# Hyena stage of a two-block transformer kernel: spectrum products in two PSUM banks, two inverse blocks side by side, signal parts block by block

## The reference

```python
def hyena(zh, p):
    B, L, _ = zh.shape                      # 1, 512, 3 * 512
    zc = cw[0] * zp[:, :-2] + cw[1] * zp[:, 1:-1] + cw[2] * zp[:, 2:] + p['hy_conv_b']
    v, x1, x2 = jnp.split(zc.astype(jnp.float32), 3, axis=-1)
    kf = jnp.fft.rfft(hyena_filters(L, p), axis=0)
    y = v
    for o, gate in enumerate((x1, x2)):
        yf = jnp.fft.rfft(y, n=2 * L, axis=1)
        conv = jnp.fft.irfft(yf * kf[:, o][None], n=2 * L, axis=1)[:, :L]
        y = gate * (conv + skip[o] * y)
    return y.astype(zh.dtype)
```

## Time and profile before

| | us |
|---|---|
| median of 3 runs | 3689.84 (3687.9 to 3692.53) |
| the profiled execution, its time | 3695.89 |
| its span, first to last instruction | 3694.1 |
| TensorE busy | 3524.5 (95% of the span) |
| DVE busy | 2093.1 (57%) |
| ACT busy | 1383.3 (37%) |
| POOL busy | 1831.8 (50%) |
| first product of the Hyena projection to last inverse product | some 1800 to 1983 |

### The profile page before, as it was taken

One profiled execution on the slowest core, in us unless ns is written; L12 is line 12 of the kernel. 1 busy time (PEld: TensorE's weight loads), 2 busy tenths in 40 slices (PEclk: granted clock), 3 DMA queues, 4 the chain that ended last, 5 costly groups with the idle time before them and its releaser, 6 DMA issues. The chain is left out here.

```text
span 3694.1 us, 49775 instructions
## 1 busy us (share of the span) xinstructions
PE 3524.5 (95%) x17547; PEld 2994.5 (81%) x17547; DVE 2093.1 (57%) x4197; ACT 1383.3 (37%) x1941; POOL 1831.8 (50%) x909
## 2 busy tenths in 40 slices
PE   8999997999999999999989999899999999999999
PEld 5777766777777688776767776689999999999999
DVE  4553045222224344215865355459999997677776
ACT  4333234223244332223323444323345454444443
POOL 5667433223243244343333311345666666788886
PEclk9999998999999999999999999999999999999999
DMA  6997545444467289422424312694459999899996
GB/s 237 367 369 259 170 148 155 129 151 142 151 202 245 86 259 288 159 86 91 142 75 137 97 60 86 221 342 158 161 179 316 346 346 348 329 378 392 387 383 233
DMA packets 458130, 813.81 MB, mean 220 GB/s; under 512 B 31544, under 2 KB 308984, under 8 KB 455322
## 3 DMA queue, kind: packets, MB, share of 16 engines
q1 hardware_dynamic: 278416, 436.07, 35.9%
q10 hardware_dynamic: 142666, 241.11, 18.5%
q0 software_dynamic: 36864, 134.23, 9.6%
HBM read 682.84 MB, written 195.56 MB: 238 GB/s over the span
## 5 line engine op out<-in xcount | busy, mean ns | idle before, releaser
L549 POOL TENSOR_TENSOR weights_lo<-weights_raw,weights_hi 128x1024 fp32r<-128x1024 f32 x649 | 1586.8, 2450 | 1791.4 <-ACT weights_hi L1241 1665.6
L627 PE MATMUL bank<-operand_hi,weights_hi 128*128 128x512 f32 (+1 forms) x2856 | 1094.5, 383 | 51.5 <-DVE operand_lo L1985 18.1
L629 PE MATMUL bank<-operand_hi,weights_lo 128*128 128x512 f32 (+1 forms) x2856 | 1065.5, 373 | 0.0
L628 PE MATMUL bank<-operand_lo,weights_hi 128*128 128x512 f32 (+1 forms) x2856 | 1064.7, 373 | 0.0
L1241 ACT ACTIVATE weights_hi<-weights_raw 128x1024 fp32r<-128x1024 f32 x649 | 683.3, 1056 | 850.0 <-PE bank L629 530.5
L627 PEld LDWEIGHTS bank<-operand_hi,weights_hi 128*128 128x128 f32 x2856 | 542.7, 190 | 141.6 <-DVE operand_lo L1985 20.2
L628 PEld LDWEIGHTS bank<-operand_lo,weights_hi 128*128 128x128 f32 x2856 | 543.2, 190 | 74.8 <-issue 5.5
L629 PEld LDWEIGHTS bank<-operand_hi,weights_lo 128*128 128x128 f32 x2856 | 541.1, 189 | 74.7
L627 PE MATMUL bank<-expert_hi,weights_hi 128*128 128x384 f32 x1024 | 345.1, 337 | 0.0
L629 PE MATMUL bank<-expert_hi,weights_lo 128*128 128x384 f32 x1024 | 345.0, 337 | 0.0
L628 PE MATMUL bank<-expert_lo,weights_hi 128*128 128x384 f32 x1024 | 345.0, 337 | 0.0
(11 more groups left out here) (401 smaller groups left out, 4883.9 us busy)
## 6 DMA issues: line engine op xcount, KB each, us to landing
weights_raw<-in_w_ffn_gu SPq DMA_DIRECT2D x132, 512.0 KB
expert_table_v<-in_w_peer_out SPq DMA_DIRECT2D x120, 512.0 KB, 5.3
weights_raw<-in_w_peer_ahead SPq DMA_DIRECT2D x120, 512.0 KB
weights_raw<-in_w_peer_out SPq DMA_DIRECT2D x120, 512.0 KB
expert_table_u<-expert_turned ACTq DMA_DIRECT2D x360, 128.0 KB, 4.7
expert_rows<-in_w_peer_ahead ACTq DMA_DIRECT2D x82, 512.0 KB, 6.8
peer_gates<-gate_stage SPq DMA_DIRECT2D x24, 1024.0 KB
expert_gates<-peer_gates ACTq DMA_DIRECT2D x16, 1536.0 KB
```

The lines of the kernel that those rows point to most:

```text
L549: pool.tensor_tensor(LO[:, slot, :], RAW[:, slot, :], HI[:, slot, :].bitcast(F32), ALU.subtract).then_inc(sem("lo_ready"), 1)
L627: pe.matmul(out, wh, hi(k), start=(k == 0), stop=False)
L628: pe.matmul(out, wh, lo(k), start=False, stop=False)
L629: ins = pe.matmul(out, wl, hi(k), start=False, stop=(k == kc - 1))
```

## The change

Five things are altered, and nothing outside the Hyena stage:

1. `hy_z` has two buffers instead of 12 and lies elsewhere, so `signal_hi` and `signal_lo` can be written during the projection.
2. In the projection, once the four turned columns of v are there, ACT makes `signal_hi` (four instructions, before its work for c = 5) and DVE makes `signal_lo` after its work for c = 5.
3. The complex product writes to PSUM banks 5 and 6 instead of `squares`, and no DVE instruction of it reads two tensors in SBUF; two waits on `piece_made` go. ACT and DVE read the parts from these banks.
4. The first two inverse blocks run side by side: `two_blocks` does step k of both before step k+1. It needs two units at its start and frees both at its end.
5. In the first order each inverse block's gated result gets its high part (ACT) and low part (DVE) at once, not after all four.

```diff
-        HZ = place("hy_z", [P, 12, TOK], F32, W1)
+        HZ = place("hy_z", [P, 2, TOK], F32, W1 + 16384)
...
+            def two_blocks(kc, hi, lo, ready):
+
+                u0, b0 = st.step // UNIT, st.block
+                assert st.step % UNIT == 0 and kc == UNIT
+                for i in range(2):
+                    claim((b0 + i) % 4)
+                for k in range(kc):
+                    ready(k)
+                    for i in range(2):
+                        if k == 0:
+                            pe.wait_ge(sem("lo_ready"), u0 + i + 1)
+                        slot, out = (u0 + i) % RING, BANK[(b0 + i) % 4][:]
+                        wh, wl = HI[:, slot, k * P:(k + 1) * P], LO[:, slot, k * P:(k + 1) * P]
+                        pe.matmul(out, wh, hi(k), start=(k == 0), stop=False)
+                        pe.matmul(out, wh, lo(k), start=False, stop=False)
+                        ins = pe.matmul(out, wl, hi(k), start=False, stop=(k == kc - 1))
+                        if k == kc - 1:
+                            ins.then_inc(sem("pe_steps"), UNIT)
...
-                ready = pieces_of(FB)
-                for m in range(TT):
-                    block_(FB, lambda k: SPH[:, k, :], lambda k: SPL[:, k, :], ready=ready if m == 0 else None)
+                spectrum = (lambda k: SPH[:, k, :]), (lambda k: SPL[:, k, :])
+                two_blocks(FB, *spectrum, pieces_of(FB))
+                for m in range(2, TT):
+                    block_(FB, *spectrum)
...
+                if c == TT:
+                    highs_after(SH, HTM[:, 0], TT, "turned", n["turn"])
             for o in range(2):
-                if o == 0:
-                    highs_after(SH, HTM[:, 0], TT, "turned", n["turn"])
-                else:
-                    highs_after(SH, HTM[:, 0], TT, "block_free", n["freed"] - TT + 1, 1)
                 for i in range(4):
                     blocks(2, TT)
                     for j in range(2):
-                        high(SPH[:, 2 * i + j, :], SQ[:, j, :])
-                blocks(TT, FB)
+                        high(SPH[:, 2 * i + j, :], BANK[5 + j][:])
+                for t in range(TT):
+                    blocks(1, FB)
+                    if o == 0:
+                        act.wait_ge(sem("block_free"), n["freed"])
+                        act.activation(SH[:, t, :], HTM[:, 0, t, :], ACT.Copy).then_inc(sem("piece_high"), 1)
...
-                free(dve.tensor_scalar(HZ[:, c, :], bank[:], vec("b_in2", c), None, ALU.add))
+                free(dve.tensor_scalar(HZ[:, c % 2, :], bank[:], vec("b_in2", c), None, ALU.add))
...
+                if c == TT + 1:
+                    lows(SL, HTM[:, 0], SH, TT)
             for o in range(2):
-                lows(SL, HTM[:, 0], SH, TT)
...
-                    dve.wait_ge(sem("piece_made"), n["made"])
                     link(dve.tensor_tensor(t0, ar[:], kr, ALU.mult))
-                    link(dve.tensor_tensor(t1, ai[:], ki, ALU.mult))
-                    made(dve.tensor_tensor(SQ[:, 0, :], t0, t1, ALU.subtract))
-                    dve.wait_ge(sem("piece_made"), n["made"])
-                    link(dve.tensor_tensor(t0, ar[:], ki, ALU.mult))
-                    free(dve.tensor_tensor(t1, ai[:], kr2, ALU.mult), 2)
+                    link(dve.tensor_tensor(re[:], ai[:], ki, ALU.mult))
+                    made(dve.tensor_tensor(re[:], t0, re[:], ALU.subtract))
+                    link(dve.tensor_tensor(t1, ai[:], kr2, ALU.mult))
+                    free(dve.tensor_tensor(im[:], ar[:], ki, ALU.mult), 2)
                     evacuated()
-                    made(dve.tensor_tensor(SQ[:, 1, :], t0, t1, ALU.add))
+                    made(dve.tensor_tensor(im[:], t1, im[:], ALU.add))
                     for j in range(2):
-                        low(SPL[:, 2 * i + j, :], SQ[:, j, :], SPH[:, 2 * i + j, :])
+                        low(SPL[:, 2 * i + j, :], BANK[5 + j][:], SPH[:, 2 * i + j, :])
+                dve.wait_ge(sem("operand_ready"), n["operand"])
+                dve.wait_ge(sem("turned"), turns0 + 12)
                 for t in range(TT):
                     bank = done(FB)
                     free(dve.tensor_tensor(HTM[:, 0, t, :], bank[:], HTM[:, 1 + o, t, :], ALU.mult))
+                    if o == 0:
+                        low(SL[:, t, :], HTM[:, 0, t, :], SH[:, t, :])
```

More of the change, by code:

```diff
@@ L712, in blocks_together @@
                         owner[(b0 + i) % 4] = ("block_free", n["freed"])
+            def two_blocks(kc, hi, lo, ready):
[15 more added lines that the diff above has]
+                            ins.then_inc(sem("pe_steps"), UNIT)
+                st.step += UNIT * 2
+                st.told = st.step
+                st.block += 2
+                for i in range(2):
+                    n["freed"] += 1
+                    owner[(b0 + i) % 4] = ("block_free", n["freed"])
             def sum_pair(matrix, bank):
@@ L2457, in _ @@
                     dve.wait_ge(sem("turned"), turns0 + c - 1)
-                z, out = HZ[:, c, :], HCV[:, c % 2, :]
+                z, out = HZ[:, c % 2, :], HCV[:, c % 2, :]
                 link(dve.tensor_scalar(out, z, vec("cw1", c), vec("cb", c), ALU.mult, ALU.add))
@@ L2463, in _ @@
                                          ALU.mult, ALU.add).then_inc(sem("conv_ready"), 1)
-            dve.wait_ge(sem("turned"), turns0 + 12)
+                if c == TT + 1:
+                    lows(SL, HTM[:, 0], SH, TT)
             for o in range(2):
-                lows(SL, HTM[:, 0], SH, TT)
                 for i in range(4):
@@ L2472, in _ @@
                     t0, t1 = HCV[:, 0, :], HCV[:, 1, :]
-                    dve.wait_ge(sem("piece_made"), n["made"])
+                    re, im = BANK[5], BANK[6]
                     link(dve.tensor_tensor(t0, ar[:], kr, ALU.mult))
-                    link(dve.tensor_tensor(t1, ai[:], ki, ALU.mult))
-                    made(dve.tensor_tensor(SQ[:, 0, :], t0, t1, ALU.subtract))
-                    dve.wait_ge(sem("piece_made"), n["made"])
-                    link(dve.tensor_tensor(t0, ar[:], ki, ALU.mult))
-                    free(dve.tensor_tensor(t1, ai[:], kr2, ALU.mult), 2)
+                    link(dve.tensor_tensor(re[:], ai[:], ki, ALU.mult))
+                    made(dve.tensor_tensor(re[:], t0, re[:], ALU.subtract))
+                    link(dve.tensor_tensor(t1, ai[:], kr2, ALU.mult))
+                    free(dve.tensor_tensor(im[:], ar[:], ki, ALU.mult), 2)
                     evacuated()
-                    made(dve.tensor_tensor(SQ[:, 1, :], t0, t1, ALU.add))
+                    made(dve.tensor_tensor(im[:], t1, im[:], ALU.add))
                     for j in range(2):
-                        low(SPL[:, 2 * i + j, :], SQ[:, j, :], SPH[:, 2 * i + j, :])
+                        low(SPL[:, 2 * i + j, :], BANK[5 + j][:], SPH[:, 2 * i + j, :])
+                dve.wait_ge(sem("operand_ready"), n["operand"])
+                dve.wait_ge(sem("turned"), turns0 + 12)
                 for t in range(TT):
```

## The result

The changed kernel takes 3670.67 us (median of 7 runs, 3664.58 to 3679.84) against 3689.53 us before (7 runs, 3687.9 to 3701.07): a ratio of 0.9948, with an interval of 0.9938 to 0.9958. The forecast was 3668.6 us, with a range of 3663 to 3676 us. In a profile of each, the spans are 3694.1 and 3673.2 us.

The account below looks back on a forecast made before the run. TensorE, busy 95% of the span, bounds the kernel, so only its stops can move. 21.9 us gone less 0.5 + 0.25 added make 21.15 us; 3689.84 - 21.2 = 3668.6 us, range 3663 to 3676 us.

Parts of the forecast that it names:

- 2.1 was put down: First forward transform: the 2.14 us wait for signal_lo behind the last turn goes, 2.1 us gained.
- its own rule: TensorE stops anywhere: each costs its idle time plus 0.16 us.
- POOL and two SBUF inputs: Complex product: POOL holds up DVE instructions reading two SBUF tensors; with banks, 1.28 us should go from six pairs.
- The price of a bank: Complex product: DVE writing a bank instead of SBUF costs nought; a pair takes 5.6 to 5.7 us.
- The rival by which the work in banks is slower: Complex product: each instruction takes longer while TensorE writes other banks; kernel 11 us slower, 3701 us; chance 3%.
- The step with the largest terms: Inverse transforms of both orders: stops of 5.3 us each go, with 1.8 and 1.7 us of low clock.
- Between the orders: Between the two orders, parts made block by block: 3.4 us of stops gone, 0.25 left.
- The projection: Projection: DVE's early low parts make TensorE stop; 0.5 us added, bounds 0 and 1.7.
- The clock at the first forward transform: First forward transform: clock stays at its higher level behind the 2.56 us stop, 2.3 us gained.
- the rival in the prediction: First forward transform: the clock still falls, giving back 2.3 us, 3671 us; chance 12%.
- Nothing takes up what comes earlier: Behind the stage: TensorE is busy 107 of 107 us from 1993 to 2100, so nothing in sight swallows the gain.
- the shorter stop: First forward transform: by the skill's clock rule, the 2.56 us stop is safer than the 2.95 us one.

Follow-up runs that it names:

- the two later ones: The changed kernel, unaltered, timed twice more against the kernel before: medians 3669.59 us (ratio 0.9946) and, on one chip, 3673.87 us (0.9957).
- the third profile of the changed kernel: A later profile of the unaltered changed kernel: 157.74 us from first Hyena projection bias to last gate product, against 179.55 before.
- the first experiment: Changed kernel with complex products back in SBUF: 160.54 us from first projection bias to last gate product, against 159.26 in the changed kernel.
- The kernel with all three steps: Changed kernel plus last turn behind first forward block, low signal parts singly at c = 5 to 8, two output turns earlier: 3666.3 us mean.
- the changed kernel's second profile: Another profile of the unaltered changed kernel: 159.27 us from first Hyena projection bias to last gate product.

## Why the prediction was right, point by point

**The size and the sign.** 21.15 us less were summed and 20.3 measured in the stretch. Between the medians it was 18.9 us in the first measurement, 22.2 and 15.8 in the two later ones. The stops were those described: each part, undone, gave back a stop in its own stage, though for the banks not the stop that was foreseen. Part of the closeness is luck. In the third profile of the changed kernel, where the clock stayed up as forecast, 21.8 us are gone from the stretch. So the sum was 0.7 us short, the fall of the clock took 1.5 us back, and the two errors ran against each other. Of the 0.7 us, 0.3 lie ahead of the first forward product: without the fall it starts 0.41 us after the turn, 2.4 us less than the 2.80 before, where 2.1 was put down. The prediction did not apply its own rule there, that a stop costs its idle time plus 0.16 us.

**POOL and two SBUF inputs.** Right, and now shown by one instruction with its output moved alone. One reading was loose: L2476 does not end with POOL's instruction at 1890.96, but at 1889.52 + 1.98 = 1891.50. The held instructions of all the kernels with products in SBUF end 0.55 us after POOL's. The price of a bank, nought from the earlier trace rows, came out at 0.70 us against 0.69. The rival by which the work in banks is slower is refuted by the same rows.

**The inverse.** The step with the largest terms (5.3 + 1.8 and 5.3 + 1.7) measured 7.22 and 7.13 us. What the prediction did not say is that two edits were each sufficient for most of it. It put the whole of the stops down under the two blocks and gave the banks no term of their own. Taken as the price of each part, that would have been far off. In the first experiment the place was also wrong: with slow pairs the bank that comes free late is the wait, not the last piece. The prediction had checked that bank only for fast pairs (20.7 against 22.5 us).

**Between the orders.** 3.31 us against 3.15; the remainder was 0.24 us where 0.25 was worked out.

**The projection.** The term was mis-sized, within its bounds: 0.80 us instead of 0.5. The cause is a held instruction that the prediction's own working left unhindered. DVE and POOL in the projection of the changed kernel:

```profile
1836.29 0.75 DVE L2481 TENSOR_SCALAR hy_z<-bank,vectors 128x512 f32<-128x512 f32 x1
1837.07 2.41 DVE L2487 TENSOR_SCALAR hy_conv<-hy_z,vectors 128x512 f32<-128x512 f32 x1
...
1836.81 2.39 POOL L549 TENSOR_TENSOR weights_lo<-weights_raw,weights_hi 128x1024 fp32r<-128x1024 f32 x1 [3.52 <-ACT weights_hi L1267]
```

L2487 reads one tensor, in SBUF; it takes 2.41 us beside POOL instead of 0.55. The stop that TensorE makes behind it costs 0.58 + 0.16 us. The kernel with all three steps has the low parts one at a time, so DVE is not late, and there this stop and the 0.8 us are gone. Its convolution line is held nowhere (least, median and greatest of 12, in ns):

```profile
L2493 DVE TENSOR_SCALAR hy_conv<-hy_z,vectors x12: 545/547/549, 1798.8 to 1863.2; 128x512 f32<-128x512 f32 x12
```

The Trainium skill (SBUF — State Buffer, on the shared port pair) says that a `tensor_scalar` from SBUF to SBUF can enter a mode that takes both pairs of ports and then contends with POOL. The trace agrees; the stop of 0.74 us lies between the 0.3 of the prediction's own working and the 1.0 us that it worked out from that rule.

**The clock at the first forward transform.** This is the step that failed. The forecast took the clock to stay up behind a stop of 2.56 us, since it had stayed up behind one of 2.95, and gave the fall 12%. It fell in the profile (1.38 us gained instead of 2.3, and 0.4 us more between the turn and the first product), in the changed kernel's second profile and in four of the five other kernels that keep this stop with products behind it. In its third profile, and with the products in SBUF, it did not fall:

```profile
1870.26 0.66 PE L756 MATMUL bank<-identity,hy_conv 128*128 128x128 f32 x4 [2.56 <-DVE hy_conv L2490]
1870.67 0.48 PE L627 MATMUL bank<-signal_hi,weights_hi 128*128 128x512 f32 x1
1870.99 0.40 PE L628 MATMUL bank<-signal_lo,weights_hi 128*128 128x512 f32 x1
1871.22 0.40 PE L629 MATMUL bank<-signal_hi,weights_lo 128*128 128x512 f32 x1
```

These are the same instructions behind the same 2.56 us. The prediction read one trace of a matter that goes either way. The fall costs 159.26 - 157.74 = 1.5 us, where the rival in the prediction priced it at 2.3. That this rival's 3671 us is the measured median is chance, since the runs spread over 15 us.

**Behind and ahead of the stage.** "Nothing takes up what comes earlier" holds, but the profiles do not repeat. The first bias starts anywhere from 1796.65 to 1805.20 us in fourteen profiles, in code that no edit touches, and from the last gate product to the end of the span it takes 1707.9 to 1714.8 us. Before, these were 1803.54 and 1711.0; the first profile after had 1799.78 and 1714.1. So the 20.9 us between the two spans are 3.8 of luck ahead, 20.3 of the stage and 3.2 of bad luck behind. The last is the clock. At the stop of 2.95 us it fell after and not before, which cost 1.6 us, and it differs further on as well. Behind the last gate product TensorE spends 37.5 us at 1.2 GHz in the profile before. In the changed kernel's first and third profiles it spends 44.4 us there and this part takes 1714.1 and 1713.9 us; in its second it spends 23.9 us and this part takes 1707.9 us. The granted clock from 2080 to 2120 us is 0.83 in the first and third and 0.96 in the second. Over the fourteen profiles the time behind the stage follows the time at the lower clock closely (correlation 0.97); ahead of the stage it does so less (0.85). Why the clock falls in one execution and not in another stays open.

## What to carry to other kernels

Where GpSimd works beside VectorE, look for VectorE instructions that do not end until shortly after the GpSimd one does (0.55 us after it here); one input in PSUM frees a two-input instruction, whether its output goes to PSUM or to SBUF. When a producer lags a consumer, shortening the producer and reordering the consumer are substitutes: price each with the other in place and without, since the sum of the two undone alone (5.5 us) is not what they are worth together (14.1 us). Work that nobody needs yet, as the last turn here, does not belong ahead of work that is ready. Where the clock makes the whole time vary, compare a stretch of the profile, and compare whole times at the same granted clock.

## What the runs showed of the hardware that was not expected

- The granted clock behind one and the same stop is not fixed. Behind the 2.56 us ahead of the last turn it went to 1.2 GHz in six of eight profiles that have products right behind it, and stayed at 2.4 in two; the first forward transform then takes 23.5 to 23.9 us or 22.3. Behind the last stop of the stage it fell in six of the twelve profiles in which that stop is 2.9 to 3.0 us, and in both in which it is 2.1 us, so nothing here shows the shorter stop to be the safer one. One profile without a fall is no evidence that a stop is short enough.
- A VectorE instruction with a single SBUF input (`tensor_scalar`, fp32, SBUF to SBUF) was held beside GpSimd to 2.41 us instead of 0.55, once in the changed kernel; in the kernel before none of its 12 was.
- Writing a VectorE product to a PSUM bank instead of SBUF costs 0.01 us in 0.69, and ScalarE read a bank in 0.60 us instead of SBUF in 0.63, with TensorE writing other banks all the while.
- The time ahead of the stage differs by 8.6 us and the time behind it by 6.9 us from profile to profile, and the second goes with the time that TensorE spends at 1.2 GHz there: 23.9 us of it in the shortest, 47.8 in the longest.
